# A paged compression stage in nine units of 57 pages instead of 16 of 32, with its weights and first pages fetched before the stage begins

## What is computed

```python
def nsa_compress(k, pe, phi1, phi2):
    B, L, G, d = k.shape
    nc = L // NSA_BLOCK
    kb = k[:, :nc * NSA_BLOCK].reshape(B, nc, NSA_BLOCK, G, d) + pe[None, None, :, None, :]
    kb = kb.transpose(0, 1, 3, 2, 4).reshape(B, nc, G, NSA_BLOCK * d)
    return jax.nn.silu(kb @ phi1) @ phi2
...
        old = cache_kv[li, page_table, :, 0:2].reshape(B, PAST_LEN, 2, G, d)
        kc_all = jnp.concatenate([old[:, :, 0], kc], axis=1)
        vc_all = jnp.concatenate([old[:, :, 1], vc], axis=1)
    kcb = nsa_compress(kc_all, pe_k, phi1_k, phi2_k)
    vcb = nsa_compress(vc_all, pe_v, phi1_v, phi2_v)
```

## Time and profile before

| what | value |
|---|---|
| median of 3 runs | 3305.0 us (3301.87 to 3306.06) |
| the profiled execution's own time | 3311.88 us |
| its span, first to last instruction | 3310.1 us |
| mean granted TensorE clock | 0.914 of full speed |
| TensorE busy | 2873.9 us (87%) |
| DMA over the span | 321.07 MB |

### The profile page before, as it was taken

One profiled execution on the slowest core, in us unless ns is written; L12 is line 12 of the kernel. 1 busy time (PEld: TensorE's weight loads), 2 busy tenths in 40 slices (PEclk: granted clock), 3 DMA queues, 4 the chain that ended last, 5 costly groups with the idle time before them and its releaser, 6 DMA issues. The chain is left out here.

```text
span 3310.1 us, 75832 instructions
## 1 busy us (share of the span) xinstructions
PE 2873.9 (87%) x28710; PEld 1935.4 (58%) x28710; DVE 1246.8 (38%) x3269; ACT 899.0 (27%) x2155; POOL 145.2 (4%) x151
## 2 busy tenths in 40 slices
PE   6999889799994569799978999799999996877868
PEld 4555555566663534455548999767676764555534
DVE  2111455354446521110100000075757574656523
ACT  1101444343331010101000000065646463434400
POOL 0000000000006200000000000000000000111100
PEclk9999999899997589899987999798989897988979
DMA  4001000566653132511026666300000003666532
GB/s 166 24 11 43 1 1 1 179 201 196 199 154 35 26 124 71 204 42 45 32 72 212 206 206 206 86 21 2 2 2 2 2 2 93 203 205 199 184 135 87
DMA packets 312626, 321.07 MB, mean 97 GB/s; under 512 B 72404, under 2 KB 289796, under 8 KB 311945
## 3 DMA queue, kind: packets, MB, share of 16 engines
q1 hardware_dynamic: 233494, 243.35, 24.2%
q10 hardware_dynamic: 78772, 72.88, 7.3%
HBM read 289.08 MB, written 30.27 MB: 96 GB/s over the span
## 5 line engine op out<-in xcount | busy, mean ns | idle before, releaser
L2115 PE MATMUL bank<-cm_pg,cm_phi 64*64 64x64 f32 x8192 | 303.8, 330 | 2.7 <-issue 2.6
L2115 PEld LDWEIGHTS bank<-cm_pg,cm_phi 64*64 64x64 f32 x8192 | 297.2, 162 | 6.4 <-issue 5.1
L2441 ACT ACTIVATE np_p<-bank,np_nmax 128x640 f32<-128x640 f32 (+7 forms) x256 | 179.5, 701 | 222.8 <-DVE np_nmax L2496 221.4
L1966 PE MATMUL bank<-op_w,op_hT 128*128 128x512 f32 (+3 forms) x576 | 225.4, 552 | 0.0
L2380 PEld LDWEIGHTS bank<-kv,np_pT 128*64 128x64 f32 x4224 | 147.1, 140 | 88.2 <-ACT np_pT L2450 43.1
L2380 PE MATMUL bank<-kv,np_pT 128*64 128x64 f32 x4224 | 182.8, 231 | 2.3 <-ACT np_pT L2450 2.2
L2496 DVE TENSOR_REDUCE np_nmax<-bank 128x1 f32<-128x640 f32 (+7 forms) x256 | 181.2, 708 | 8.8
L315 PE MATMUL bank<-ev_hT,ev_w 128*128 128x384 f32 (+1 forms) x576 | 176.8, 467 | 6.1 <-ACT zaT L258 6.1
L2366 PE MATMUL bank<-ident,np_p 128*128 128x128 f32 x1056 | 176.9, 293 | 3.5 <-ACT np_pcT L2461 2.8
L1966 PEld LDWEIGHTS bank<-op_w,op_hT 128*128 128x128 f32 (+1 forms) x576 | 104.1, 182 | 117.6 <-issue 106.7
L2450 ACT ACTIVATE np_pT<-bank 128x512 f32<-128x512 f32 (+3 forms) x384 | 160.8, 459 | 37.9 <-PE bank L2366 37.9
(11 more groups left out here) (510 smaller groups left out, 4280.8 us busy)
## 6 DMA issues: line engine op xcount, KB each, us to landing
ms_pg<-cache_mla SPq DMA_DIRECT2D x384, 144.0 KB, 2.8
ns_pg<-cache_nsa_kv SPq DMA_DIRECT2D x384, 128.0 KB, 2.7
cm_pg<-cache_nsa_kv ACTq DMA_DIRECT2D x256, 128.0 KB, 4.3
cm_pg<-cache_nsa_kv SPq DMA_DIRECT2D x256, 128.0 KB, 3.6
ms_pg<-cache_mla ACTq DMA_DIRECT2D x128, 144.0 KB, 2.6
ns_pg<-cache_nsa_kv ACTq DMA_DIRECT2D x128, 128.0 KB, 3.0
ev_w<-w_in_even SPq DMA_DIRECT2D x8, 768.0 KB, 10.2
op_w<-w_in_odd SPq DMA_DIRECT2D x24, 256.0 KB, 6.5
```

The lines of the kernel that those rows point to most:

```text
L1966: t = nc.tensor.matmul(bank[:n, f, 0:hi - lo], hT[:, i // 3 % 2, k, at:at + n], w[:, k, NW + lo:NW + hi], start=k == 0, stop=k == KD - 1)
L2115: t = nc.tensor.matmul(out(blk)[kind * HD:(kind + 1) * HD], phi[blk * BLK:(blk + 1) * BLK, kind, x, :], rows(kind, blk, x), start=x == 0, ...
L2441: nc.scalar.activation(p[:, u % NPS, :width(u)], scores_ps(u)[:, :width(u)], ACT.Exp, bias=nmax[:, u % NST:u % NST + 1], accum_out=den[:, ...
```

## The change

- `compress` works in nine units of `CU` = 57 pages (the last has 56), cut through the list of all 512 pages, so that a unit can hold the end of one sequence and the start of the next. The matmuls of L2115 get 114 columns instead of 64.
- A unit that crosses a border is passed through SiLU in two pieces (`segments`); `products` runs once for a sequence instead of twice, with 64 columns for keys and 64 for values, after the first unit behind the sequence's end.
- There are two page buffers instead of three. The load of unit n waits until unit n - 2 is multiplied; now the reading of the table stands behind that wait too. SP fetches 29 pages of a unit and ScalarE 28, each with two readings of the table.
- One tensor, `early["room"]`, is shared by the two stages. `odd_projection` lays its arrays into it, with the weights split into `wt` (token chunks) and `wq` (queries). What it needs last lies behind `wt`, `x` and `h`.
- When ScalarE has done its last gate of `odd_projection`, it issues all weight loads of `compress` (`phi_load`) and the first `soon` = 45 pages of unit 0 into the room of `wt`, `x` and `h`. The other 12 pages of unit 0 follow on its queue at the start of `compress`; SP begins with unit 1.

```diff
-def odd_projection(nc, a, d, c, o):
+def odd_projection(nc, a, d, c, o, early):
...
+        wt = place(KD * ODD_TOK).rearrange("p (k n) -> p k n", k=KD)
+        x = place(NX * D_MODEL).rearrange("p (x n) -> p x n", x=NX)
+        h = place(2 * D_MODEL).rearrange("p (x n) -> p x n", x=2)
+        soon = (at - PHI_EL) // (2 * KVW)
+        wq = place(KD * NW).rearrange("p (k n) -> p k n", k=KD)
...
                     for i in range(3 * x3 + 3, min(3 * x3 + 6, len(tiles))):
                         squares(i)
+                for half_ in range(2):
+                    phi_load(act, a, early, half_)
+                phi_pages(nc, act, mybir.EngineType.Activation, a, c, early, 0, 0, soon)
...
+PHI_EL = 2 * HD * HD
+CU = 57
+CP = DB * NPAGE
...
+def phi_load(eng, a, early, half):
+    phi = phi_room(early)[0]
+    rows = slice(half * BLK, (half + 1) * BLK)
+    for kind, p1 in enumerate(("nsa_phi1_k", "nsa_phi1_v")):
+        eng.dma_start(phi[rows, kind], a[p1][0].rearrange("(r x) m -> r x m", x=HD)).then_inc(early["s_w"], 16)
+    eng.dma_start(early["phi2"][rows], a[("nsa_phi2_k", "nsa_phi2_v")[half]][0]).then_inc(early["s_w"], 16)
+    eng.dma_start(early["pe"][:, half, :], a[("nsa_pe_k", "nsa_pe_v")[half]][0]).then_inc(early["s_w"], 16)
+
+
+def phi_pages(nc, eng, kind, a, c, early, n, lo, hi):
+
+    pg = phi_room(early)[1]
+    for first in range(lo, hi, 16):
+        last = min(first + 16, hi)
+        _, pages = nc.values_load_multi_w_load_instructions(c["pages"][0:1, n * CU + first:n * CU + last], engines=[kind], min_val=0, max_val=POOL - 1)
+        for j, page in enumerate(pages, first):
+            eng.dma_start(pg[:, n % 2, j, :], a["cache_nsa_kv"][0, ds(page, 1)].rearrange("a p k g d -> (a p) (k g d)")[:, 0:2 * KVW]).then_inc(early["s_page"][n % 2], 16)
...
+        def load(eng, kind, n, lo, hi):
+            if n >= 2:
+                eng.wait_ge(S["acc"], n - 1)
+            phi_pages(nc, eng, kind, a, c, early, n, lo, hi)
...
             def _(sp):
-                load_weights(sp, 0)
-                for n in range(NN):
-                    load_half(sp, SP, 0, n)
+                for n in range(1, NU):
+                    load(sp, SP, n, 0, sizes[n] - sizes[n] // 2)
...
             def _(act):
-                load_weights(act, 1)
-                for n in range(NBUF):
-                    load_half(act, AC, 1, n)
+                load(act, AC, 0, early["soon"], CU)
+                load(act, AC, 1, CU - CU // 2, CU)
                 act.wait_ge(S["bias"], 1)
...
-                for n in range(NN):
+                for i, (n, b, at, page, count) in enumerate(segments):
                     act.wait_ge(S["acc"], n + 1)
-                    if n >= 2:
-                        act.wait_ge(S["out"], n - 1)
-                    nc.scalar.activation(hid[:, n % 2], bank[:, 2 * (n % 2):2 * (n % 2) + 2, 0:2 * HP], ACT.Silu, bias=bias[:]).then_inc(S["hid"], 1)
-                    if n + NBUF < NN:
-                        load_half(act, AC, 1, n + NBUF)
+                    if b >= 2:
+                        act.wait_ge(S["out"], b - 1)
+                    nc.scalar.activation(hid[:, b % 2, :, 2 * page:2 * (page + count)], bank[:, 2 * (n % 2):2 * (n % 2) + 2, 2 * at:2 * (at + count)],
+                                         ACT.Silu, bias=bias[:]).then_inc(S["hid"], 1)
+                    if i + 1 == done[n] and n + 2 < NU:
+                        load(act, AC, n + 2, sizes[n + 2] - sizes[n + 2] // 2, sizes[n + 2])
...
+                ready = 0
+                for n, size in enumerate(sizes):
+                    pe.wait_ge(s_page[n % 2], 16 * sum(sizes[n % 2:n + 1:2]))
                     if n >= 2:
-                        pe.wait_ge(S["hid"], n - 1)
+                        pe.wait_ge(S["hid"], done[n - 2])
...
+                    while ready < DB and n >= 1 and (ready + 1) * NPAGE <= n * CU:
+                        products(ready)
+                        ready += 1
```

More of the change, by code:

```diff
@@ L2085, in sb @@
             return ctx.enter_context(nc.sbuf_tensor(name, shape, F32))
[L2087 to L2089 removed]
+        phi, pg = phi_room(early)
+        phi2, pe_sb, s_w, s_page = (early[k] for k in ("phi2", "pe", "s_w", "s_page"))
         bias = sb("cm_bias", [P, 1])
[L2091 to L2092 removed]
+        hid = sb("cm_hid", [P, 2, 2, 2 * NPAGE])
         hidp = sb("cm_hidp", [P, 2, NC])
[L2094 removed]
         names = ["bias", "acc", "hid", "out", "ev", "dv", "accp", "biasd", "hidp", "outp", "evp"]
         S = {n: cleared(nc, ctx, "cm_s_" + n) for n in names}
[L2098 removed]
         SP, AC = mybir.EngineType.SP, mybir.EngineType.Activation
[L2101 to L2108, removed]
+        segments = []
+        for n, size in enumerate(sizes):
+            at = n * CU
+            while at < n * CU + size:
+                b = at // NPAGE
+                to = min((b + 1) * NPAGE, n * CU + size)
+                segments.append((n, b, at - n * CU, at - b * NPAGE, to - at))
+                at = to
+        ends = {b: max(i for i, x in enumerate(segments) if x[1] == b) + 1 for b in range(DB)}
+        done = {n: max(i for i, x in enumerate(segments) if x[0] == n) + 1 for n in range(NU)}
+        def load(eng, kind, n, lo, hi):
+            if n >= 2:
+                eng.wait_ge(S["acc"], n - 1)
+            phi_pages(nc, eng, kind, a, c, early, n, lo, hi)
         def hidden(out, rows):
@@ L2169, in _, with products @@
                 t.then_inc(S["outp"], 1)
[L2171 to L2178, removed]
+                def products(b):
+                    pe.wait_ge(S["hid"], ends[b])
+                    pe.wait_ge(S["evp"], 2)
+                    if b >= 1:
+                        pe.wait_ge(S["ev"], 4 * b)
                     for half in range(2):
@@ L2186, in products @@
                                 else:
-                                    t = nc.tensor.matmul(bank[hf * HP:(hf + 1) * HP, 6 + half, gg * HD:(gg + 1) * HD], cols, phi2[rows, :], start=True, stop=True)
+                                    t = nc.tensor.matmul(bank[:NPAGE, 6 + half, gg * HD:(gg + 1) * HD], cols, phi2[rows, :], start=True, stop=True)
                     t.then_inc(S["out"], 1)
-                for n in range(NN):
-                    for queue in range(2):
-                        pe.wait_ge(s_half[n % NBUF][queue], 16 * QP * (n // NBUF + 1))
+                ready = 0
@@ L2204, in _ @@
+                while ready < DB:
+                    products(ready)
+                    ready += 1
             @block.vector
```

69 lines of the change are left out of this document (36 added, 33 removed).

## The result

The median went from 3302.32 us (8 runs) to 3284.01 us (8 runs, 3274.94 to 3291.10): a ratio of 0.9947, 95% interval 0.9929 to 0.9964, so 18 us faster (12 to 23). Timed once more it was 0.9911 (0.9878 to 0.9944), 30 us. Forecast were 3271, so 34 us less, in a range of 3210 to 3292.

The account below looks back on a forecast made before the run. TensorE was taken to bound the loop of 332.3 us, by reading far-apart columns. Saving 8.4 us before the bias and 25.2 in the loop, 33.6 in all, gave 3271 us, range 3210 to 3292.

Parts of the forecast that it names:

- own range: Whole kernel: 3255 to 3284 us, from the hold, 0.3 to 1.8 us a call and small waits for loads.
- rival 3: Compression stage: smaller gain, products stay at 1.8 us a call and the hold eats the head; 3287 us; chance 0.10.
- three signs of being wrong: 114 columns cost well under 1.78 times 64; TensorE waits for pages from the third unit on; first activation comes late.
- Reading (a): Cached pages' matmuls: price per column, from reading columns 64 floats apart; 33.3 us a unit, 298 us against 299.0.
- Rivals 1 and 2: Cached pages' matmuls: price part fixed (3236 us, chance 0.17) or mostly fixed (3206 us, chance 0.11).
- Products and gaps: Loop: products 0.8 us a call instead of 1.8, 4.8 plus 2.0 in all; gaps 2.3 instead of 4.0.
- The head: Before the loop: ScalarE's early issues hold the barrier; bias starts at 1734 against 1742.48, 8.4 us saved.
- ends at 1770, just before it is needed: Before the loop: ScalarE's tables and page issues queued ahead of the activations end at 1770; lateness beyond 1771 is lost.
- Hidden by 2 to 4 us: Loop, two buffers: a load takes 30 to 32 us behind 33.3 + 0.8 us of TensorE work, at no cost.
- Rival 4: Loop: a load's two halves come one behind the other in two buffers, load 58 us; 60 us lost; chance 0.07.
- The prediction's own condition: Loop: if a unit took less than a load (L), the period would be (unit + L)/2.
- The sum: Whole kernel: 8.4 us before the bias and 25.2 in the loop make 33.6 saved; median 3271 us.

Follow-up runs that it names:

- neighbouring columns: The changed kernel, but the 57-page matmuls read 114 neighbouring floats as columns instead of columns 64 floats apart (other numbers multiplied): 3220.78 us, one run.
- table ahead of the wait: The changed kernel, but the first reading of a unit's page table goes ahead of the wait for the free buffer, on both queues: 3272.55 us, ratio 0.9884.
- after, again: The changed kernel unaltered, timed once more: 3277.15 us, ratio 0.9911 to the kernel before.
- early fetch undone: The changed kernel, but weights and all pages of unit 0 are issued at the start of the compression stage, half on each queue: 3289.90 us, ratio 0.9941.
- column distances: The changed kernel, but units 0 to 8 read columns 64, 32, 16, 8, 4, 2, 1, 64, 64 floats apart: 3280.95 us, one run.
- 16 early: The changed kernel, but only 16 pages fetched early, the other 41 shared by SP and ScalarE, both activations ahead of unit 1's loads: 3267.32 us, one run.

## Why the prediction was right, and where it was off

The median lies in the range, at the upper end of the own range of 3255 to 3284, with just over half of the saving that was forecast. By the median alone rival 3 (3287) is nearer than the forecast; it is the trace that decides for the forecast, with 30.4 us saved in the stage. Two of the three signs of being wrong that the prediction named did appear: the first activation came late, and TensorE waited for pages from the third unit on.

**Matmuls.** Reading (a) held: 33.0 us a unit against 33.3, 64.3 ns against 36.5, a ratio of 1.76 at 1.78 times the columns; 297.0 us in all against 298. Its reason, told there as a limit on reading far columns, is shown by the neighbouring columns and by the distances. Rivals 1 and 2 fall with it. The fixed part that they take is not seen, and the weight loads do not set the round of four quarters: with neighbouring columns 283 matmuls, each with its own load, go at 24.7 ns, 99 a round.

**Products and gaps.** 0.57 a call, not 0.8; the change of tile shape was most of the price, as assumed: with it a call takes 1.94 us again. The gaps between instructions, 2.3 in the sum, are nearly gone. Together this is some 5 us better than forecast; rival 3 falls. That the loop as a whole is so close to its forecast (306.1 against 307.1) is luck: the waits for pages, put at nothing, take back the same 5 us.

**The head.** Right: the barrier held by ScalarE's early issues. The last one came at 1726.8, which is 1730.7 on the clock of the earlier trace rows (where the odd projection ended 3.9 later), against 1731; the bias started at 1733.7 there, against 1734. The step that was off is "ends at 1770, just before it is needed". ScalarE's 40 pages with three tables were put at 36.1 us from the start of the stage and took 40.9 (1729.80 to 1770.7). The readings of the table took longer: the first page came 5.4 us after the bias had started, not 3.6, and the pauses before the second and third row of issues were 7.2 and 5.5, not 4.8 and 3.6. The issues themselves, 22.8 us, were no slower than the 24.1 forecast. And TensorE was done sooner: the own rows ended 32.4 us after the bias had started, against 36.6 before, since the idle times marked issue between their matmuls fell from 8.3 to 4.1 us. So the activation was 9.14 late and the loop began at 1776.1 on the clock of the earlier trace rows, not 1772.

**Two buffers.** "Hidden by 2 to 4 us" failed. Unit 0 was multiplied at 1805.3, unit 2 started at 1841.55: L = 36.3 against 28 to 32, with 34.1 of cover forecast. On SP's queue the parts are:

```profile
1812.90 22.64 SPq L2114 DMA_DIRECT2D cm_room<-cache_nsa_kv  x29
```

7.6 until the first page (4.8 forecast), 22.6 of pages with the second table (19 to 22.5), and 6.0 until the last has landed (4.1, a median where the last of 57 counts). Rival 4's mechanism, two halves one behind the other, did not show: both queues began at 1812.9. The prediction's own condition, a load longer than a unit, explains what was paid: three loads ended after the unit that was to hide them, which cost 5.5 us in all. Reading the table ahead of the wait took these waits away (table ahead of the wait).

**The sum.** Stage 30.4 saved, 33.6 forecast: 0.4 better before the bias, 4.5 lost up to the loop, 0.9 better in the loop. In the first comparison the medians differ by only 18, in the second by 30. In the kernels with intervals the medians moved as the stages did: 30.0 us for 29.1 (after, again), 20.7 for 17.7 (early fetch undone), 44.3 for 40.9, 21.1 for 18.4, 34.6 for 36.1, 60.4 for 61.0. In the three changed kernels that were executed once the times moved less than the stages: 89.8 for 96.2 (neighbouring columns), 21.0 for 41.3 (column distances), 34.6 for 51.9 (16 early). In the two traced executions the span shrank by 24.8, 5.6 less than the stage: the prompt's attention was 6.0 longer and the sampled sequences' 3.3, and what lies ahead of the stage 3.9 shorter. I take the first comparison's shortfall for such wandering, above all of the clock granted in the prompt's attention; that is argued and not shown for those eight runs, and whether the change has a part in it stays open.

## What to carry to other kernels

Ask of a small matmul what its price hangs on before cutting it wider: an equal count at both clock levels says that the array's clock isn't the limit. Here the limit was the reading of far columns, and then width gives nothing and layout gives much. Ahead of a short instruction that another engine waits for, no list of DMA issues should stand; an early fetch is worth having only as far as its issues end before the barrier. With fewer buffers, everything that needs no buffer (here the reading of addresses) belongs ahead of the wait, and the slowest landing counts, not the median.

## What the runs showed of the hardware beyond that

- Float columns 4 to 16 apart cost TensorE 1.8 times what columns 1 or 2 apart cost (50 against 27 ns for 114 columns), and 64 apart 2.3 times (64 ns).
- A change between 64x64 and 64x32 tiles cost some 0.13 us. The Trainium skill (TensorEngine Tiling (Array Packing), Key Properties) says that a change of tiling mode drains the engine; the call of 1.94 us against 0.57 agrees.
- Reading 16 page addresses into registers and starting the first page took 4.8 us during the odd projection (1684.27 to 1689.09 on ScalarE) and 7.0 to 7.6 in the loop (7.0 from the end of ScalarE's activation, 7.6 on SP from the end of unit 0); why was not tried.
